# Griffin and mLSTM streaming step on one core: hidden forms loaded straight into the operand buffers, three of the seven split while they are made, squares on ScalarE, norm scale and residual applied once per row

## The reference

```python
x = x + mix @ w_out
hmlp = jax.nn.relu(rmsnorm(x, norm_mlp) @ w_up)      # 1024 -> 4096
x = x + (hmlp * hmlp) @ w_down                        # 4096 -> 1024
```

## Time and profile before

| | us |
|---|---|
| median of 3 runs | 2244.49 (2243.88 to 2245.09) |
| profiled execution, its own time | 2242.76 |
| its span | 2241.0 |
| PE busy | 2157.6 (96%) |
| DVE, POOL, ACT busy | 1519.6 (68%), 1154.0 (51%), 667.8 (30%) |
| channel mixer, first product to the last phase | about 1475 to 2128 |

### The profile page before, as it was taken

How to read it: one execution, slowest core, us unless ns; L and a number is a source line. 1 busy time by engine, 2 the same in 40 slices (tenths; PEclk the granted TensorE clock), 3 DMA queues, 4 the chain that set the end, 5 groups by cost and what they waited for, 6 DMA issues and landing times.

```text
span 2241.0 us, 37284 instructions
## 1 busy us (share of the span) xinstructions
PE 2157.6 (96%) x14230; PEld 2129.1 (95%) x14230; DVE 1519.6 (68%) x1578; ACT 667.8 (30%) x850; POOL 1154.0 (51%) x785
## 2 busy tenths in 40 slices
PE   7999999999999999999999998979999999898998
PEld 6999999999999999999999998979999999898988
DVE  6576767165757667676757546477777678988856
ACT  4443434113223232323232202232222242433322
POOL 4556555342424334243424334458777778787761
PEclk9999999999999999999999999999999999999999
DMA  3212113421211112121212124423434554434322
GB/s 123 67 58 66 58 57 104 148 95 39 76 59 52 55 47 64 43 68 43 64 47 74 33 87 133 128 82 118 158 118 154 182 199 167 149 106 126 114 62 81
DMA packets 88609, 207.53 MB, mean 93 GB/s; under 512 B 8880, under 2 KB 14128, under 8 KB 87504
## 3 DMA queue, kind: packets, MB, share of 16 engines
q1 hardware_dynamic: 62992, 132.58, 18.8%
q10 hardware_dynamic: 25536, 73.83, 9.6%
HBM read 157.03 MB, written 49.34 MB: 92 GB/s over the span
## 4 chain that ended last, share of the span: by engine, by line
PE 76%; DVE 14%; issue 6%; ACT 3%; DMA 1%; DVEq 0%; POOL 0%; POOLq 0%; ACTq 0%; SPq 0%
PE ps L808 43%; PE ps L1031 21%; PE ps L1130 4%; DVE vt L1708 2%; PE ps L929 2%; DVE acc L1711 2%; DVE form_lo L1711 2%; PE ps L957 1%; DVE tmp L1711 1%; PE ps L975 1%; PE ps L978 1%; DVE snap L1711 1%; ACT vt L1140 1%; DVE xm_lo L1711 1%; PE ps L983 1%
## 5 line engine op out<-in xcount | busy, mean ns | idle before, releaser
L686 POOL TENSOR_TENSOR w_hi<-w_raw,ones 128x512 fp32r<-128x512 f32 x218 | 267.6, 1228 | 831.7 <-PE ps L808 803.6
L808 PE MATMUL ps<-u_hi,w_hi 128*128 128x364 f32 x1560 | 348.1, 331 | 16.9 <-POOL w_lo L689 9.6
L689 POOL TENSOR_TENSOR w_lo<-w_raw,w_hi 128x512 fp32r<-128x512 f32 x218 | 348.8, 1600 | 17.1
L808 PE MATMUL ps<-u_hi,w_lo 128*128 128x364 f32 x1560 | 344.8, 329 | 0.0
L808 PE MATMUL ps<-u_lo,w_hi 128*128 128x364 f32 x1560 | 344.3, 329 | 0.0
L808 PEld LDWEIGHTS ps<-u_hi,w_hi 128*128 128x128 f32 x1560 | 271.1, 189 | 19.4 <-issue 10.7
L808 PEld LDWEIGHTS ps<-u_lo,w_hi 128*128 128x128 f32 x1560 | 271.7, 188 | 0.0
L808 PEld LDWEIGHTS ps<-u_hi,w_lo 128*128 128x128 f32 x1560 | 271.6, 188 | 0.0
L1031 PE MATMUL ps<-form_hi,hi 128*128 128x274 f32 x784 | 168.9, 298 | 28.6 <-DVE small L1711 17.0
L1031 PE MATMUL ps<-form_hi,w_hi 128*128 128x274 f32 x776 | 164.0, 293 | 6.2 <-DVE small L1711 5.8
L1031 PE MATMUL ps<-form_lo,hi 128*128 128x274 f32 x784 | 167.5, 296 | 0.0
(11 more groups left out here) (286 smaller groups left out, 4510.9 us busy)
## 6 DMA issues: line engine op xcount, KB each, us to landing
w_raw<-in_w SPq DMA_DIRECT2D x290, 256.0 KB, 2.6
stage<-hid_forms SPq DMA_DIRECT2D x42, 548.0 KB, 3.9
rstd<-in_w SPq DMA_DIRECT2D x42, 256.0 KB, 2.6
hid_forms<-acc ACTq DMA_DIRECT2D x12, 822.0 KB, 6.6
bc<-out_rows ACTq DMA_DIRECT2D x8, 1092.0 KB, 6.1
hid_forms<-stage ACTq DMA_DIRECT2D x6, 1096.0 KB, 4.4
hid_forms<-acc ACTq DMA_DIRECT2D x6, 1096.0 KB, 4.4
acc<-in_x_t SPq DMA_DIRECT2D x8, 546.0 KB, 8.0
```

The lines of the kernel that those rows point to most:

```text
L686: nc.gpsimd.tensor_tensor(w_hi[:, c, :], w_raw[:, c, :], one, ALU.mult).then_inc(s_whi, 1)
L689: nc.gpsimd.tensor_tensor(w_lo[:, c, :], w_raw[:, c, :], w_hi[:, c, :].bitcast(F32), ALU.subtract).then_inc(s_wlo, 1)
L808: mm = nc.tensor.matmul(slots[slot][:, t, :], w, r(k)[:, t * TW:(t + 1) * TW], start=(k == 0 and n == 0), stop=(k == last_k and n == 2))
```

## The change

- **Hidden data, up projection.** DVE no longer squares. ACT does, with two instructions for a quarter (`relu2`: Relu, then Square). The sums of a unit move behind its end: DVE makes the three sums that need three quarters at the start of the next unit, ahead of P4's quarter (`hid_sums`, then `hid21`), and the fourth after the next unit's two partial sums (`hid_rest`).
- **Three forms split while they are made.** For T1, T2 and T4 ACT rounds (`sum_hi`) and DVE subtracts (`sum_lo`). A unit stores ten pieces with four DMAs (`store`, now one place earlier in the order), of which `KEPT` = 10 stand for a group in `forms_d`.
- **Loads, down projection.** ACT starts them. B11, B21, T3 and B22 are loaded with one DMA of 1096 KB into the low tile itself, ACT rounds from there, DVE subtracts in place. T1, T2 and T4 are loaded with two DMAs, high and low, and nothing else is done to them. Each load waits for the last product of the old group that reads the tile. `stage`'s ring is gone.
- **Norm scale and residual.** The first down group writes its quarters straight into `acc` (`direct`), the others only add (`mixed`), and a row of 1092 columns is once multiplied by the scale and has the residual added (`row`): rows 0 to 3 in G6, rows 4 to 7 in the last phase. SP loads the residual rows one at a time.
- **First unit.** ACT makes the scaled upper halves for T3 earlier, and the copy of the first partial later; DVE adds up the squares of the last row after T3; P2's quarter moves behind B22, and T4's sums and splits are interleaved block by block.
- **Last phase.** Weight chunks 10 to 15 lie elsewhere, and chunk 10 waits for the last product.

```diff
 STORED = {B11: 0, T3: 1, B21: 2, B22: 3, T1: 4, T2: 5, T4: 6}
+STORED_HI = 3
+KEPT = FORMS + 3
...
         def by_pair(v):
 
-            return lambda f, k: LO_AT[v, f, k // 2] if k % 2 == 0 else None
+            def waits(f, k):
+                if f in SPLIT:
+                    return [split_in(v, f)] if k == 0 else []
+                return [(s_nlo, LO_AT[v, f, k // 2])] if k % 2 == 0 else []
+            return waits
...
         def store(group, r):
 
-            act.wait_ge(h_step, 8 * (4 * group + r) + 8)
-            for src, first, n in ((hid_q[r % 2], 0, 4), (hid_t[r % 2], 4, 3)):
-                dst = forms_d[bass.ds(FORMS * group + first, n)][:, :, r, :]
+            act.wait_ge(h_step, FORMS * (4 * group + r) + 7)
+            th, t_hi2 = hid_h[r % 2]
+            for src, first, n in ((hid_q[r % 2], 0, 4), (hid_t[r % 2], 4, 3), (th, 7, 2), (t_hi2, 9, 1)):
+                dst = forms_d[bass.ds(KEPT * group + first, n)][:, :, r, :]
                 act.dma_start(dst.rearrange("f p c -> p f c"), src).then_inc(h_st[r % 2], 16)
...
+        def relu2(group, r, i):
+
+            u, ap = 4 * group + r, hid_out(group, r)[(0, 3, 1, 2)[i]]
+            act.wait_ge(s_q, QUARTERS * u + (3, 4, 6, 7)[i])
+            a(ap, ap, ACT.Relu, h_sq)
+            act.wait_ge(h_sq, 8 * u + 2 * i + 1)
+            a(ap, ap, ACT.Square, h_sq)
...
+            act.dma_start(form[f][1][:].bitcast(F32), forms_d[KEPT * (v - 1) + STORED[f]])\
+                .then_inc(raw_in(v, i)[0], 16)
...
+            for part in range(2):
+                src = forms_d[KEPT * (v - 1) + STORED[f] + (0 if part else STORED_HI)]
+                act.dma_start(form[f][part][:].bitcast(F32), src).then_inc(done, 16)
...
+            def between(step):
+                if step == 0:
+                    relu2(*prev, 2)
+                    sum_hi(*prev, 0)
+                    relu2(*prev, 3)
+                    sum_hi(*prev, 1)
+                elif step == 1:
+                    sum_hi(*prev, 2)
+                elif step == 2:
+                    store(*prev)
+                elif step in (3, 4):
+                    relu2(group, r, step - 3)
...
+                if (r, step) == (2, 5):
+                    load_raw(v, 0)
+                elif (r, step) == (3, 1):
+                    raw_hi(v, 0)
+                    act.wait_ge(s_mm, index(group, r, P5) + 1)
+                    load_split(v, T1)
...
+                elif (r, step) == (3, 5):
+                    raw_hi(v, 1)
+                elif (r, step) == (3, 6):
+                    raw_hi(v, 2)
+                    act.wait_ge(s_mm, index(group, r, P3) + 1)
+                    load_raw(v, 3)
...
+            if (r, step) == (0, 1) and v > 1:
+                raw_hi(v - 1, 3)
+                act.wait_ge(s_mm, index(group, r, P5))
+                load_split(v - 1, T4)
...
+        def up_unit(group, r, prev, extra=None):
+            q = hid_out(group, r)
             extra = extra if extra is not None else (lambda step: None)
+            hid_sums(*prev)
+            hid21(*prev)
+            sum_lo(*prev, 0)
+            dve.wait_ge(s_q, QUARTERS * (4 * group + r))
             partials(group, r)
+            hid_rest(*prev)
             for stored_hid, count in hid_free(group, r):
                 dve.wait_ge(stored_hid, count)
-            hid11(group, r, q[0])
+            quarter(group, r, P2, q[0], snap1[:], 2)
...
+        def row(n):
+
+            dve.wait_ge(g_in[n % 2], 128 + 16 * (n // 2) + 16)
+            tt(acc[:, n, :], acc[:, n, :], tmp[:, 3, :], ALU.mult, f_row)
+            dve.wait_ge(f_row, 2 * n + 1)
+            tt(acc[:, n, :], acc[:, n, :], stage[:, n % 2, 0:COLS], ALU.add, f_row)
```

More of the change, by code:

```diff
@@ L133 @@
 PRODUCTS = FORMS * UNITS
-ADDS = 8
+ADDS = 4
 QUARTERS = 7
+RAW, SPLIT = (B11, B21, T3, B22), (T1, T2, T4)
 def form_counts(first_blocks):
@@ L309, in build @@
     hid_t = [quarters(acc_flat, 0, 3), quarters(acc_flat, 7, 3)]
+    hid_h = [(quarters(acc_flat, 10 + 2 * j, 2), quarters(stage[:].rearrange("p a c -> p (a c)"), 4 + j, 1))
+             for j in range(2)]
     raw11, raw12, raw21 = w_raw[:, 0, :], w_raw[:, 1, :], rstd[:, 0:CHUNK]
@@ L1025, in multiply @@
             for k in range(4):
-                if ready is not None and ready(f, k) is not None:
-                    pe.wait_ge(s_nlo, ready(f, k))
+                if ready is not None:
+                    for made, count in ready(f, k):
+                        pe.wait_ge(made, count)
                 w_h, w_l = (w[:, k * P:(k + 1) * P] for w in (w_his[s], w_los[s]))
@@ L1509, in _ @@
         a(w_his[2], wsum[:], ACT.Copy, v_hi)
+        for j in range(1, 4):
+            upper_half(j)
+        square(KB - 1)
+        act.wait_ge(r_raw12, 16)
+        a(w_his[3], raw12, ACT.Copy, v_hi)
         act.wait_ge(s_mm, 1)
@@ L1512, in _ @@
         copy1(0, pairs[0])
-        square(KB - 1)
-        act.wait_ge(r_raw12, 16)
-        a(w_his[3], raw12, ACT.Copy, v_hi)
-        for j in range(4):
-            a(t4_f[:, j, :], acc[:, j, SECOND], ACT.Copy, o_e, scale=gain2(j))
         keep(KB - 1)
@@ new lines, in load_split, with raw_hi @@
+        def load_split(v, f):
+            done, count = split_in(v, f)
+            if count > 32:
+                act.wait_ge(done, count - 32)
+            for part in range(2):
+                src = forms_d[KEPT * (v - 1) + STORED[f] + (0 if part else STORED_HI)]
+                act.dma_start(form[f][part][:].bitcast(F32), src).then_inc(done, 16)
+        def raw_hi(v, i):
+            done, count = raw_in(v, i)
+            act.wait_ge(done, count)
+            for half in range(2):
+                hi, lo = (form[RAW[i]][part][:, 2 * half:2 * half + 2, :] for part in range(2))
+                a(hi, lo.bitcast(F32), ACT.Copy, s_nhi)
@@ L2308, in _, with first_unit @@
-        up_unit(0, 0, first_extra)
+            quarter(group, r, P3, q[1], snap4, 2)
+            extra(2)
+        def first_unit():
+            q = hid_q[0]
+            partials(0, 0)
+            for j in range(4):
+                lo_scaled(B22, j, acc[:, 4 + j, SECOND], 4 + j)
+            quarter(0, 0, P2, q[:, 0, :], snap1[:], 2)
+            combine4(0)
+            for j in range(4):
+                if j < 3:
+                    combine4(j + 1)
+                dve.wait_ge(o_t, 16 + 2 * j + 2)
+                lo_plain(T4, j, t4_f[:, j, :])
+            quarter(0, 0, P7, q[:, 3, :], snap4, 2)
+            quarter(0, 0, P7, snap2[:], snap2[:], 1)
+            quarter(0, 0, P3, q[:, 1, :], snap4, 2)
@@ new lines, in _, with direct @@
+            quarter(group, r, P7, q[3], snap4, 2)
+            quarter(group, r, P7, snap2[:], snap2[:], 1)
+            dve.wait_ge(h_sq, 8 * u + 2)
+            quarter(group, r, P3, q[1], snap4, 2)
+            operands(group, r, 4)
+            operands(group, r, 5)
+        dve.wait_ge(h_sq, 8 * u + 4)
+        hid21(group, 3)
+        def direct(group, r, product, n, half, part, count, over):
+            mm_done(group, r, product)
+            dve.wait_ge(s_q, QUARTERS * (4 * group + r) + max(count, over))
+            tt(as2(acc[:, n, (FIRST, SECOND)[half]]), bank(group, r, product), as2(part), ALU.add, s_q)
@@ L2386, in mixer_add, with mixed @@
+        def mixed(u, part, half, n, count, done):
+            dve.wait_ge(s_q, QUARTERS * u + count)
             if half:
@@ L2389, in mixer_add @@
                 tt(acc[:, n, FIRST], acc[:, n, FIRST], part, ALU.add, h_add)
-            dve.wait_ge(h_add, ADDS * (u - 4 * UP_GROUPS) + done + 1)
-        def mixed(u, part, half, n, count, done):
-            dve.wait_ge(s_q, QUARTERS * u + count)
-            tt(part, part, tmp[:, 3, (FIRST, SECOND)[half]], ALU.mult, h_add)
-            mixer_add(u, done, part, half, n)
-        for group in range(UP_GROUPS, ALL_GROUPS):
+            dve.wait_ge(h_add, ADDS * (u - 4 * UP_GROUPS - 4) + done)
@@ L2419, in _ @@
+                operands(group, r, 5)
+                if group == ALL_GROUPS - 1 and r in (1, 2):
+                    row(2 * r - 2)
+                    row(2 * r - 1)
         dve.wait_ge(s_mm, PRODUCTS)
@@ L2457, in _ @@
                 last_block(t, n)
+                if t == 0 and n < 4:
+                    row(4 + n)
                 if n:
```

402 lines of the change are left out of this document (202 added, 200 removed).

## The result

The changed kernel takes **2275.52 us** (median of 4 runs, 2274.51 to 2280.72) where the kernel before took 2244.18 beside it (2242.56 to 2245.09): a ratio of 1.0137, 95% interval 1.0124 to 1.015. It is slower by 31 us; forecast were 13.5 us. The profiled execution spans 2274.3 us, 33.3 more than that of before. PE has as many matmuls as before and nearly the same busy time (2166.7 us for 2157.6); DVE has 121 us less work and ACT 75 more, and neither was what the time hung on.

The account below looks back on a forecast made before the run. PE, busy 96% of the span, bounds the kernel, with 50 us of losses to win; -5.3 + 13 + 8.5 + 5.3 - 6 - 2 = +13.5 on 2242.76 gives 2256.3, with 1.7 for the median 2258 us; range 2237 to 2278.

Parts of the forecast that it names:

- The sign and the mechanism: Kernel slower by 13.5 us, chiefly by a loop of waits in the up projection, 22.8 us against PE's 21.4.
- Up projection, +13: Twelve units each run at the loop's pace, less 4 us of weights prepared ahead: +13 us (0 to +30).
- four store issues, two being 0.95, 1.9: Link of the up projection's loop on ACT, ahead of P4's weights: four issues take 1.9 us.
- Rival (c): Up projection: all DVE instructions of the loop meet POOL, 24.3 us a unit, 31 instead of 13: 2276; chance 0.14.
- Without the loop nothing is lost: Up projection: without the loop of waits the twelve splits and squares would cost nothing.
- First unit of G3, +8.5: DVE waits for G2's last store, which lands later; P4 waits 5 to 6.5 us: +8.5 (+3 to +12).
- First unit of G0, -5.3: DVE has less ahead of T4, so P5 of unit 1 comes near 1512.9: -5.3 us (-8 to -1).
- G3 to G4, +5.3: End of group: T4's late load, one more store, ACT's squares and P4's quarter lose 10.5 for 5.2 us: +5.3.
- the other two ends, -6: G4 to G5 and G5 to G6: T4 5.4 us late plus low clock, 14 for 8.6 + 11.4: -6.
- Last phase, -2: PE hardly waits for the last hidden rows, but POOL's sixteen chunks limit the gain: -2 us (-6 to +2).
- the term for `row`: Last phase: eight 1092-column instructions beside POOL take the port for 1.2 us each.
- What would show it: Signs: up-projection gaps of 1 to 2 us released by POOL, about 1880 matmuls in 255 us, P5 near 1513.

Follow-up runs that it names:

- e5: Changed kernel with two of a unit's four store issues moved behind P2's weights, the other two left ahead of P4's weights: 2252.84 us, ratio 1.0034.
- e2: Changed kernel with the store moved behind P2's weights in units 1 and 2 of G0 alone: 2270.41 us, ratio 1.0114.
- e1: Changed kernel with all four store issues moved behind P2's weights in all up units but the first of G3: 2252.12 us, ratio 1.0031.
- e9: Changed kernel with the squares of the hidden quarters back on DVE: 2257.09 us, ratio 1.0052.
- e10: Changed kernel with DVE's low parts of three sums in the up projection cut to 2 columns (result no longer right): 2253.88 us, ratio 1.0037.
- e6: Kernel with the store behind P2's weights, G3's hidden quarters put in other rows of acc: 2246.24 us, ratio 1.0001.
- e3: Changed kernel with SP loading the second unit's first weight block ahead of the block in the squares' row: 2275.49 us, ratio 1.0125.
- e4: Changed kernel with scale and residual of rows 2 and 3 moved from G6's third unit to the last phase: 2276.75 us, ratio 1.0133.

## Why the prediction was right or wrong

**The sign and the mechanism** were right: slower, by a ring of waits in the up projection that starts at ACT's squares and goes through the store that stands ahead of P4's weights. The time lay in the range, near its upper end; the size was short by more than half. My forecast's steps one by one:

- **Up projection, +13, measured +32.3**, above its bound of +30. Two steps failed. (1) The turn was taken as 22.8 us and was 23.7. The term "four store issues, two being 0.95, 1.9" was 3.4, 1.5 us short (e5), since four in a row are not twice two; POOL's four instructions, put at 6.14, took 5.1 (1710.40 to 1715.54), which hid part of it, and the sums and the splits came out as counted (4.28 and 4.15 for 4.13 and 4.1). By the prediction's rule the twelve turns would have been 12 x 2.3 - 4 = 24 us, 11 more. (2) `norm_out` was missed: the store was put behind the last split and nothing was said of what is queued behind it on ACT besides P4's weights. That cost 9 us in units 1 and 2 (e2). Moving the store leaves 6.0 us lost in these two, for 1.4 before, with a wait of 2.27 us at the same copy and a clock of 0.76 behind the first unit's end; the prediction's sum has two of its turns in their place. Rival (c), 2276, met the time, but by another cause: DVE's instructions did not all meet POOL (0.90, 1.70, 1.70, 0.71, 0.72, 1.62 and 1.81 us in the turn shown). Its price was wrong too: it takes 24.3 us for a turn in which all meet POOL, where the prediction's own sum for that case is 26.
- **Without the loop nothing is lost**: right (e1, e5, e9, e10 lose 1.1 to 3.4 us in 213, most of it in unit 2).
- **First unit of G3, +8.5, measured +8.7**: right in place, wait (6.25 for 5 to 6.5) and clock (0.80); e6 shows it by taking the wait away.
- **First unit of G0, -5.3, measured -0.8**, just outside its bound of -1. The step that failed: "its wait for ACT's square of the last row" was counted as gone, but the sum of that square moved behind T3, and SP's queue waits for it. The prediction asked what would be late next on DVE, not on SP. SP's order accounts for 2.4 to 2.8 of the missing 4.5 us (e3). T4's last rounding came at 1512.50 where I had 1509.4, and P5 of unit 1 at 1516.44 where I had 1512.9.
- **G3 to G4, +5.3, measured +1.9; the other two ends, -6, measured -15.1.** The loads did better than the one queue I put them in: T4's load was waited for 1.17 and 0.47 us at two ends and not at all at the third, not 5.4 each (two other executions did wait 3.9 and 4.4; see below). What PE waited for at G3 to G4 was P2's weights (4.16 us, POOL), which the prediction held under 1 us: their rounding stands behind B21's on ACT.
- **Last phase, -2, measured +6.3**, above its bound of +2. The failed step is the term for `row`: it counted only what the eight instructions of the last phase take from POOL (1.2 us each), and not that four more stand on DVE ahead of the last hidden rows' low parts (7.2 us, 2133.37 to 2140.5), which is what PE waits for.
- **What would show it**: the gaps, their releaser and their place were as said; 1743 matmuls in 245 us would be 1814 in 255, where I had 1880. P5 of unit 1 was 3.5 us later than said.

**T4's load at G5 to G6** was in time, or nearly, in twelve profiled executions with the change and 4 us late in two (e3 and e10), whose code is the same there. PE's wait for it in e3 and in the changed kernel:

```profile
2086.45 0.49 PE L1025 MATMUL ps<-form_hi,hi 128*128 128x274 f32 x2 [3.94 <-DMA form_lo<-hid_forms]
```

```profile
2084.44 0.49 PE L1018 MATMUL ps<-form_hi,hi 128*128 128x274 f32 x2 [0.47 <-DMA form_lo<-hid_forms]
```

The timelines differ in the order of two queues. SP starts two loads of residual rows (546 KB each) at about the time at which ACT starts T4's two. In e3 SP's first goes out ahead of ACT's second, in the changed kernel behind it. SP and ACT in e3, then ACT and SP in the changed kernel:

```profile
2073.92 0.84 SPq L622 DMA_DIRECT2D stage<-residual  x2
2074.14 0.47 ACTq L1588 DMA_DIRECT2D form_lo<-hid_forms  x1
```

```profile
2075.20 0.46 ACTq L1581 DMA_DIRECT2D form_lo<-hid_forms  x1
2075.39 0.84 SPq L615 DMA_DIRECT2D stage<-residual  x2
```

The two late executions are the only ones of the fourteen in this order (e10: 2048.51 and 2048.88). That the row load is what makes T4 late fits all of them, but no run moved it on purpose, so the cause is likely and not shown. It is as large as the effects that e3 and e4 were to show, and one reason why a single profiled execution says little of 4 us.

## What to carry to other kernels

When a step moves later on an in-order engine, list everything that is queued behind it, on that engine and on the queue that waits for its result, the once-only instructions too: here a store and a sum held up things that the change did not touch (`norm_out`, SP's weight block), and in e4 a row load held up the chunks. An engine that is idle for 40% of the time can still close a ring. Sum the ring, not the engines, and then break it at its cheapest link: moving one store to a place where nobody waits gave back 23 us. Measure a row of issues as a row, for four of them cost 3.4 us and not twice the 0.95 of two. And repair before you discard: with its orders repaired the change is a gain (0.9947) where as written it was a loss (1.0137).

## What the runs showed of the hardware

- DMA issues in a row on ACT's queue are not equally dear: two took 0.94 us, three 2.10 and four 3.43 in the loop, and two in unit 1 took 2.98. The third and the fourth of a store, issued later by themselves, took 0.38 and 0.35 (e5).
- Taking a wait away from POOL made DVE slower: four low parts of 548 columns took 7.02 us in place of 4.80 (e3).
- Loads that two queues start within half a us of each other can land some 4 us apart from one execution to the next: T4's was waited for 3.94 and 4.38 us in the two executions in which a row load on SP's queue went out ahead of its second half, and 0 to 1.4 us in the twelve others.
